# Two-block transformer on one core: side panels' weights split behind a unit's normalisation in the two-map attention

## The chip, the cores and the metric

The kernel runs on one core of a Trainium2 chip. The metric is the device time of one execution in microseconds; of several executions the median counts.

## The reference

256 tokens of width 1024 go through two blocks, all in float32. The first block (two layers: gated feed-forward, three kinds of attention, a second gated feed-forward) is not touched here. The second block computes, cut to what matters:

```
h = rmsnorm(x); p = h @ w_in
p_rwkv, p_mla, p_diff, p_gate = split(p)
o_rwkv = rwkv7_mix(p_rwkv)       # recurrent branch, with a group norm at its end
o_mla  = mla_mix(p_mla)          # latent attention, 8 heads
o_diff = diff_mix(p_diff)        # 4 heads; softmax of map 1 minus lambda * softmax of map 2
gates  = sigmoid(p_gate + b)     # 3 x 1024 columns
merged = sum over the branches of gate * (o_branch @ w_branch)
x = x + merged @ w_o; x = x + conv_ffn(rmsnorm(x)); return rmsnorm(x)
```

## The kernel before

**Panels and splits.** Every weight matrix is streamed from HBM in panels of 128 x 2048 floats. A float32 product is made of three fast ones (`three`, lines 1214 to 1216): high half of the weights by high half of the tokens, high by low, low by high. So a panel that has landed in `raw` must be split first: ScalarE (ACT) copies it to `whi` in the reduced format, VectorE (DVE) subtracts, which gives `wlo`. The rest of the kernel does this a whole panel at a time (`split`, lines 581 and 585). `split_piece` (lines 588 to 611) does it in four pieces: 0 and 2 are the two halves of `whi` (lines 598 and 600), 1 and 3 the two halves of `wlo` (both line 608). A panel's first matmul waits until piece 3 of that panel is done. The load of a panel into a `raw` slot waits until the slot's previous `wlo` is done.

**Side panels.** The projection `h @ w_in` has 27 panels of side work (`side_list`). They aren't multiplied in a stage of their own: they are put between the small, dependent steps of the branches, to fill the matmul engine (TensorE, PE). A panel is four quarters of 12 matmuls of 256 columns each. `dense(k)` issues the next k quarters. The generator `side_panels` issues for each quarter its matmuls (`side_quarter`), in a panel's quarter 0 also the copy of the panel before out of its bank (`side_flush`, `side_evac`, line 2249 for gate columns), and right behind the quarter the split of the next panel. From panel 16 on the split comes in pieces: behind quarter 0 piece 0, behind quarter 1 pieces 1 and 2, behind quarter 2 piece 3, behind quarter 3 none.

**Two-map attention.** `causal_attention` is a generator that takes one unit (a head and a block of 128 queries; 8 units) per turn. For unit i:

```
if n_maps == 2 and i + 1 < len(units):
    scores(i + 1)            # PE, at the head of turn i+1; both maps, banks 4 and 5
exponentials(i)              # DVE adds the bias map (L2886) and takes the maxima (L2798), ACT exponentials (L2800)
normalise(i - 1)             # DVE, L2809 to L2817
transposes(i - 2)            # PE (L2826), then an ACT copy (L2830)
values(i - 3)                # PE (L2890, L2891)
```

`scores(i + 1)` (L2879) waits for the exponentials of unit i, since both use banks 4 and 5. `transposes(i - 2)` waits for that unit's normalisation and for the copy of the transposes before.

**The order around the change.** The loop at the end of `second_block` takes 8 turns. In each: a unit's step; in turn 0 `dense(2)`; then one step of the recurrent branch's epilogue (`group_norm`) or, when that is over, of `mla_inputs` (the MLA heads' queries and keys: PE L2917 and L2919, ACT L2922 to L2928, DVE L2931 to L2935); then `dense(1 + i % 2 + (i == 1))`. When the loop starts, panel 16 has two quarters behind it. Panels 17, 18, 19 and 20 start in turns 0, 2, 5 and 7. Each engine works through its own instructions in the order in which they were issued, so what is written first also runs first on its engine.

Of the kernel before, what the change touches and what calls it, by code (L numbers as in the profile page):

```python
# [748 lines left out]
def build(nc, ins, out):  # L749
# [1420 lines left out]
    side_list = [("rwkv_in", k) for k in range(7)] + [("diff_in", k) for k in range(6)] + \  # L2170
                [("mla_in", k) for k in range(2)] + [("gate_in", k) for k in range(12)]
    s_side = nc.alloc_semaphore("side_panel_evacuated")
    mixed, side_at, side_quarters = {}, [0], [0]
# [14 lines left out]
    def side_quarter(n, q):  # L2188

        name, k = side_list[n]  # L2190
        g = PHASE[name].first + k
        slot, b = g % 2, q // 2
        if q == 0:
            pe.q.wait_ge(st.s_lo, g + 1)
            if n >= 3:
                pe.q.wait_ge(s_side, n - 1)
        if n == 0:
            for kc in range(2 * q, 2 * q + 2):
                r = high_first([(side_target(0, b), tile_of(slot, b * KC + kc), S) for b in range(2)], u_one, kc, ready[kc])[1]
        for kc in range(4 * (q % 2), 4 * (q % 2) + 4) if n else ():  # L2200
            if name == "diff_in" and k >= 4:
                w = (whi[slot][:, kc * 256:(kc + 1) * 256], wlo[slot][:, kc * 256:(kc + 1) * 256])
                r = three(side_target(n, b), chunk_of(u_one, kc, b * P, b * P + P), w, kc == 0, kc == KC - 1)
            else:
                r = three(side_target(n, b), tile_of(slot, b * KC + kc), chunk_of(u_one, kc, 0, S), kc == 0, kc == KC - 1)
        if q == 3:
            r.then_inc(st.s_pe, 1)
# [44 lines left out]
    def side_panels():  # L2252

        for n in range(len(side_list)):
            for q in range(4):
                side_quarter(n, q)
                if q == 0 and n >= 1:
                    side_flush(n)
                name, k = side_list[n + 1] if n + 1 < len(side_list) else ("branch", 0)
                if n < 16:  # L2260
                    if q == 0 and n > 0:
                        st.split(PHASE[name], Count(k))
                else:
                    for piece in ((0,), (1, 2), (3,), ())[q]:
                        st.split_piece(PHASE[name], k, piece)
                yield
        side_flush(len(side_list))

    def side_flush(n):

        if side_at[0] < n:
            side_evac(n - 1)
            side_at[0] = n

    side = side_panels()

    def dense(quarters):
        for _ in range(quarters):
            next(side, None)
            side_quarters[0] += 1  # L2280

    def side_done(name, k):
        n = side_list.index((name, k))
        assert side_at[0] > n, (name, k)
        return (s_side, n + 1)
# [29 lines left out]
    for i in range(4):  # L2315
        dense(2)
        x2 = scaled_rows("norm_final", [], range(2 * i, 2 * i + 2))
# [451 lines left out]
    def causal_attention(name, units, score, prepare, n_maps, pv, stat, free, probs, probs_t, twin, before):  # L2769


        mk = [dict() for _ in units]

        def score_bank(i, m):
            return banks[4 + m if n_maps == 2 else 4 + i % 2][:, 0:S]

        def scores(i):
            uu = units[i]
            j = i - 1 if n_maps == 2 else i - 2
            pe.after(mk[j]["exp"] if j >= 0 else before.get("exp"))  # L2780
            for m in range(n_maps):
                r = score(uu, m, score_bank(i, m))
            mk[i]["scores"] = pe.do(r)
            if name == "diff":
                gates_free[uu[0]] = gates_free[4 + uu[0]] = mk[i]["scores"]

        def exponentials(i):
            uu = units[i]
            qt = uu[-1]
            nk = (qt + 1) * P  # L2790
            k = i % 2
            st_ = stat[:, k, :]
            dve.after(mk[i]["scores"], mk[i - 2]["norm"] if i >= 2 else None)
            act.after(mk[i - N_PROBS]["transposed"] if i >= N_PROBS else None)
            for m in range(n_maps):
                bank = score_bank(i, m)
                dve.after(prepare(uu, m, bank))
                t = dve.do(dve.q.tensor_reduce(out=st_[:, m:m + 1], in_=bank[:, 0:nk], axis=AX.X, op=ALU.max, negate=True))  # L2798
                act.after(t)
                ex = act.do(act.q.activation(probs[i % N_PROBS][:, m, 0:nk], bank[:, 0:nk], ACT.Exp, bias=st_[:, m:m + 1],  # L2800
                                             accum_out=st_[:, 2 + m:3 + m]))
            mk[i]["exp"] = twin["exp"] = ex

        def normalise(i):
            nk = (units[i][-1] + 1) * P
            k = i % 2
            st_ = stat[:, k, :]
            dve.after(mk[i]["exp"])
            t = dve.do(dve.q.reciprocal(st_[:, 4:4 + n_maps], st_[:, 2:2 + n_maps]))  # L2809
            dve.after(t)  # L2810
            if n_maps == 2:
                t = dve.do(dve.q.tensor_tensor(st_[:, 5:6], st_[:, 5:6], lam[:, 3:4], ALU.mult))
                dve.after(t)
            t = dve.do(dve.q.tensor_scalar(probs[i % N_PROBS][:, 0, 0:nk], probs[i % N_PROBS][:, 0, 0:nk], st_[:, 4:5], None, ALU.mult))
            if n_maps == 2:
                dve.after(t)
                t = dve.do(dve.q.scalar_tensor_tensor(out=probs[i % N_PROBS][:, 0, 0:nk], in0=probs[i % N_PROBS][:, 1, 0:nk],  # L2817
                                                      scalar=st_[:, 5:6], in1=probs[i % N_PROBS][:, 0, 0:nk],
                                                      op0=ALU.mult, op1=ALU.add))
            mk[i]["norm"] = t  # L2820

        def transposes(i):
            qt = units[i][-1]
            pe.after(mk[i]["norm"], turned_free.get("copied"))
            for t in range(qt + 1):
                r = pe.q.transpose(banks[0][:, t * P:(t + 1) * P], probs[i % N_PROBS][:, 0, t * P:(t + 1) * P], cst("ident"))  # L2826
            mk[i]["transposed"] = pe.do(r)
            pair = i // 2
            act.after(mk[i]["transposed"], mk[2 * (pair - 2) + 1]["pv"] if pair >= 2 else None)
            mk[i]["copied"] = turned_free["copied"] = act.do(act.q.activation(  # L2830
                probs_t[pair % 2][:, 0:qt + 1, qt * P:(qt + 1) * P],
                banks[0][:, 0:(qt + 1) * P].rearrange("p (t q) -> p t q", t=qt + 1), ACT.Copy))

        def values(i):
            if units[i][-1] == 0:
                return
            pair = i // 2
            bank = banks[1][:, 0:S]
            pe.after(mk[i]["copied"], mk[i - 1]["copied"], turned_free.get("read"))
            r = pv(units[i], probs_t[pair % 2], bank)  # L2840
            mk[i]["pv"] = pe.do(r)
            if name == "diff":
                for t in range(2):
                    gates_free[8 + 2 * (pair // 2) + t] = mk[i]["pv"]
            free[pair] = turned_free["read"] = finish_head(name, units[i], bank, mk[i]["pv"])

        scores(0)
        for i in range(len(units) + 3):
            if n_maps == 1 and i + 1 < len(units):
                scores(i + 1)  # L2850
            if i < len(units):
                exponentials(i)
            if 1 <= i <= len(units):
                normalise(i - 1)
            if 2 <= i < len(units) + 2:
                transposes(i - 2)
            if i >= 3:
                values(i - 3)
            yield
            if n_maps == 2 and i + 1 < len(units):  # L2860
                scores(i + 1)
# [118 lines left out]
    def mla_pv(uu, pt, bank):  # L2980
# [10 lines left out]
    diff_heads = causal_attention("diff", diff_units, diff_score, diff_prepare, 2, diff_pv, diff_stat, diff_free,  # L2991
                                  diff_probs, diff_probs_t, last_of, {})
    builder = None
    for i in range(len(diff_units)):
        next(diff_heads)
        if i == 0:
            dense(2)
        if builder is None:
            if next(epilogue, "over") == "over":
                builder = mla_inputs()  # L3000
        if builder is not None:
            next(builder, None)
        dense(1 + i % 2 + (i == 1))
    mla_units = [(hh, qt) for hh in range(MH) for qt in range(2)]
    mla_heads = causal_attention("mla", mla_units, mla_score, mla_prepare, 1, mla_pv, mla_stat, mla_free,
                                 mla_probs, mla_probs_t, {}, last_of)
# [185 lines left out]
```

## Time and profile before

| | us |
|---|---|
| median of 3 runs | 2327.96 |
| the runs | 2321.61 to 2328.72 |
| the profiled execution, its own time | 2326.03 |
| its span, first to last instruction | 2324.7 |
| mean granted clock of TensorE in it | 0.989 |

Busy in the profiled execution: PE 2260.5 us, PE's weight loads 1920.7, DVE 1490.9, ACT 964.4, POOL 393.9. The attention that the change touches runs from 1945 to 1998 us of the span. A duration in the rows is that of one instruction or of a merged group; "idle before" is the time that the engine stood still ahead of it, and behind the arrow stands what ended that.

### The profile page before, as it was taken

The numbers are of one execution on the slowest core, as the hardware profiler recorded it, in microseconds if no ns is written. First come the engines' busy times: TensorE is split into PE (matmuls) and PEld (weight loads), VectorE is DVE, ScalarE is ACT, GpSimd is POOL, SyncE is SP. The second block draws the span as 40 slices with busy tenths as digits, with TensorE's granted clock in tenths as the row PEclk, the third lists the DMA queues.
The fourth block names the chain that finished last, engine by engine and source line by source line (L and its number), as shares of the span: only waits on it lengthen the run. The fifth ranks groups of instructions, "written<-read, shape, count | busy, mean of one in ns | idle before, by whom it ended". The sixth has DMA issues, their size and how long they took to land. (4 is left out here: it accounts for less than half of the span.)

```text
span 2324.7 us, 37251 instructions
## 1 busy us (share of the span) xinstructions
PE 2260.5 (97%) x14432; PEld 1920.7 (83%) x14432; DVE 1490.9 (64%) x2302; ACT 964.4 (41%) x1555; POOL 393.9 (17%) x381
## 2 busy tenths in 40 slices
PE   9999999999999999999999999989999999999998
PEld 6888887666778888888888876679998998898998
DVE  5756766465676666676564345666667766777874
ACT  5222224455442222242222244554446335656763
POOL 1000001100010000000000011049996575000000
PEclk9999999999999999999999999999999999999999
DMA  7654543311234444434443323124554332244544
GB/s 297 221 187 162 180 162 129 106 37 55 73 118 181 171 173 161 170 139 163 162 180 130 100 103 108 58 89 178 178 175 157 110 103 91 77 157 159 189 165 143
DMA packets 53911, 331.05 MB, mean 142 GB/s; under 512 B 6688, under 2 KB 7968, under 8 KB 23328
## 3 DMA queue, kind: packets, MB, share of 16 engines
q1 hardware_dynamic: 50336, 319.15, 38.6%
q0 software_dynamic: 3456, 10.25, 1.6%
q8 instruction: 83, 1.36, 0.2%
q14 instruction: 36, 0.29, 0.0%
HBM read 325.56 MB, written 3.80 MB: 142 GB/s over the span
## 5 line engine op out<-in xcount | busy, mean ns | idle before, releaser
L1214 PE MATMUL bank<-u_hi,whi 128*128 128x512 f32 (+1 forms) x2352 | 805.2, 342 | 4.8 <-ACT qT L1716 1.6
L1215 PE MATMUL bank<-u_lo,whi 128*128 128x512 f32 (+1 forms) x2352 | 789.7, 336 | 0.0
L1216 PE MATMUL bank<-u_hi,wlo 128*128 128x512 f32 (+1 forms) x2352 | 789.6, 336 | 0.0
L585 DVE TENSOR_TENSOR wlo<-raw,whi 128x2048 fp32r<-128x2048 f32 (+2 forms) x203 | 423.6, 2086 | 307.5 <-ACT whi L581 297.8
L1214 PEld LDWEIGHTS bank<-u_hi,whi 128*128 128x128 f32 x2352 | 443.1, 188 | 82.3 <-issue 27.8
L581 ACT ACTIVATE whi<-raw 128x2048 fp32r<-128x2048 f32 (+2 forms) x203 | 345.5, 1702 | 346.3 <-PE bank L1216 296.0
L1216 PEld LDWEIGHTS bank<-u_hi,wlo 128*128 128x128 f32 x2352 | 443.3, 188 | 47.5
L1215 PEld LDWEIGHTS bank<-u_lo,whi 128*128 128x128 f32 x2352 | 442.9, 188 | 44.6 <-issue 0.2
L1289 ACT ACTIVATE sil<-bank 128x512 f32<-128x512 f32 (+1 forms) x88 | 48.0, 545 | 519.4 <-PE bank L1216 516.6
L1214 PE MATMUL bank<-hidden_hi,whi 128*128 128x512 f32 x528 | 205.4, 389 | 0.0
L1215 PE MATMUL bank<-hidden_lo,whi 128*128 128x512 f32 x528 | 205.4, 389 | 0.0
L1216 PE MATMUL bank<-hidden_hi,wlo 128*128 128x512 f32 x528 | 205.4, 389 | 0.0
L643 POOL TENSOR_TENSOR wlo<-raw,whi 128x512 fp32r<-128x512 f32 x16 | 21.4, 1335 | 971.6 <-ACT whi L627 971.5
L943 DVE SCALAR_TENSOR_TENSOR bank<-raw,c_row 128x1024 f32<-128x1024 f32 x128 | 157.2, 1228 | 8.5 <-DMA raw<-in_stream 7.4
L1407 POOL TENSOR_TENSOR rel_bias_map<-rel_bias_map,bucket_step 128x384 f32<-128x384 f32 x124 | 158.1, 1275 | 10.4
L943 DVE SCALAR_TENSOR_TENSOR raw<-raw,bank 128x1024 f32<-128x1024 f32 x128 | 155.7, 1217 | 0.0
L1293 DVE TENSOR_TENSOR prod<-sil,bank 128x512 f32<-128x512 f32 (+1 forms) x88 | 54.6, 621 | 157.3 <-ACT sil L1289 154.3
L608 DVE TENSOR_TENSOR wlo<-raw,whi 128x1024 fp32r<-128x1024 f32 (+2 forms) x84 | 99.3, 1193 | 73.3 <-ACT whi L598 69.7
L1404 POOL TENSOR_SCALAR bucket_step<-in_bucket,bucket_steps 128x384 f32<-128x384 f32 x124 | 131.5, 1060 | 12.4
L1216 PEld LDWEIGHTS bank<-hidden_hi,wlo 128*128 128x128 f32 x528 | 99.1, 188 | 20.7
L1215 PEld LDWEIGHTS bank<-hidden_lo,whi 128*128 128x128 f32 x528 | 99.1, 188 | 20.6
L1214 PEld LDWEIGHTS bank<-hidden_hi,whi 128*128 128x128 f32 x528 | 99.1, 188 | 20.4
(450 smaller groups left out, 3204.9 us busy)
## 6 DMA issues: line engine op xcount, KB each, us to landing
raw<-in_stream SPq DMA_DIRECT2D x229, 1024.0 KB, 4.8
raw<-in_stream SPq DMA_DIRECT2D x80, 704.0 KB, 4.0
first_ada<-in_stream SPq DMA_DIRECT2D x8, 1024.0 KB, 16.7
raw<-in_stream SPq DMA_DIRECT2D x8, 768.0 KB, 4.2
skew<-rpb_rows POOLq DMA_DIRECT2D x8, 336.0 KB, 6.3
nbr_bias<-skew POOLq DMA_DIRECT2D x24, 112.0 KB, 5.9
h<-in_tokens SPq DMA_DIRECT2D x4, 512.0 KB, 5.6
raw<-in_stream SPq DMA_DIRECT2D x8, 256.0 KB, 16.8
```

The lines of the kernel that those rows point to most:

```text
L581: a.activation(self.hi[to][:, 0:n], raw[:, 0:n], ACT.Copy).then_inc(self.s_hi, 1)
L585: v.tensor_tensor(self.lo[to][:, 0:n], raw[:, 0:n], self.hi[to][:, 0:n].bitcast(F32), ALU.subtract).then_inc(self.s_lo, 1)
L608: r = v.q.tensor_tensor(self.lo[to][:, cols], self.raw[slot][:, cols], self.hi[to][:, cols].bitcast(F32), ALU.subtract)
L643: r = v.q.tensor_tensor(self.lo[to][:, cols], self.raw[slot][:, cols], self.hi[to][:, cols].bitcast(F32), ALU.subtract)
L943: r = dve.q.scalar_tensor_tensor(out=product, in0=w, scalar=1.0, in1=rows, op0=ALU.mult, op1=ALU.mult, accum_out=to)
L1214: pe.q.matmul(dst, w[0], x[0], start=start, stop=False)
L1215: pe.q.matmul(dst, w[0], x[1], start=False, stop=False)
L1216: return pe.q.matmul(dst, w[1], x[0], start=False, stop=stop)
L1289: act.q.activation(sil[par][:, 0:n], banks[2 * par][:, 0:n], ACT.Silu).then_inc(s_sil, 1)
L1293: dve.q.tensor_tensor(prod[par][:, 0:n], sil[par][:, 0:n], banks[2 * par + 1][:, 0:n], ALU.mult).then_inc(st.s_ev, 1)
L1404: z = pool.do(pool.q.tensor_scalar(step[:, :], bucket[:, :], 1.0 - start, steps[:, hh, b + 1:b + 2], ALU.add, ALU.mult))
L1407: z = pool.do(pool.q.tensor_tensor(rel[:, hh, :], rel[:, hh, :], step[:, :], ALU.add))
```

## The change

The splits leave `side_panels` and get a generator of their own, `side_splits`; `next_weights` catches it up with the quarters that have been issued. Outside the two-map attention `dense` calls it behind each quarter, as before. Within it (`weights_apart`) it is called in the next turn of `causal_attention`, behind `exponentials(i)` and `normalise(i - 1)` and ahead of `transposes(i - 2)`, and by `dense` ahead of a panel's quarter 0, since that panel's split must be issued by then.

```diff
--- before.py
+++ after.py
@@ -2256,6 +2256,13 @@
                 side_quarter(n, q)
                 if q == 0 and n >= 1:
                     side_flush(n)
+                yield
+        side_flush(len(side_list))
+
+    def side_splits():
+
+        for n in range(len(side_list)):
+            for q in range(4):
                 name, k = side_list[n + 1] if n + 1 < len(side_list) else ("branch", 0)
                 if n < 16:
                     if q == 0 and n > 0:
@@ -2264,7 +2271,6 @@
                     for piece in ((0,), (1, 2), (3,), ())[q]:
                         st.split_piece(PHASE[name], k, piece)
                 yield
-        side_flush(len(side_list))
 
     def side_flush(n):
 
@@ -2272,12 +2278,22 @@
             side_evac(n - 1)
             side_at[0] = n
 
-    side = side_panels()
+    side, side_weights, split_quarters, weights_apart = side_panels(), side_splits(), [0], [False]
+
+    def next_weights():
+
+        while split_quarters[0] < side_quarters[0]:
+            next(side_weights, None)
+            split_quarters[0] += 1
 
     def dense(quarters):
         for _ in range(quarters):
+            if side_quarters[0] % 4 == 0:
+                next_weights()
             next(side, None)
             side_quarters[0] += 1
+            if not weights_apart[0]:
+                next_weights()
 
     def side_done(name, k):
         n = side_list.index((name, k))
@@ -2852,6 +2868,8 @@
                 exponentials(i)
             if 1 <= i <= len(units):
                 normalise(i - 1)
+            if weights_apart[0]:
+                next_weights()
             if 2 <= i < len(units) + 2:
                 transposes(i - 2)
             if i >= 3:
@@ -2991,6 +3009,7 @@
     diff_heads = causal_attention("diff", diff_units, diff_score, diff_prepare, 2, diff_pv, diff_stat, diff_free,
                                   diff_probs, diff_probs_t, last_of, {})
     builder = None
+    weights_apart[0] = True
     for i in range(len(diff_units)):
         next(diff_heads)
         if i == 0:
@@ -3001,6 +3020,8 @@
         if builder is not None:
             next(builder, None)
         dense(1 + i % 2 + (i == 1))
+    weights_apart[0] = False
+    next_weights()
     mla_units = [(hh, qt) for hh in range(MH) for qt in range(2)]
     mla_heads = causal_attention("mla", mla_units, mla_score, mla_prepare, 1, mla_pv, mla_stat, mla_free,
                                  mla_probs, mla_probs_t, {}, last_of)
```

In the rows of order that follow, line numbers of the change are 16 (epilogue) or 18 (attention) above those of before for the same code. `wlo<-raw,whi` on DVE is piece 1 or 3, `whi<-raw` on ACT piece 0 or 2.

DVE, between unit 0's and unit 1's mask addition, where panel 17 starts (`token_roots` and `inverse_t` belong to the epilogue's group norm). Before:

```order
L2886 TENSOR_TENSOR bank<-bank,rel_bias_map 128x128
L2798 TENSOR_REDUCE diff_stat<-bank 128x1
L608 TENSOR_TENSOR wlo<-raw,whi 128x1024
L2735 RECIPROCAL token_roots<-token_roots 128x16
L2737 COPY inverse_t<-token_roots 128x1024
L2886 TENSOR_TENSOR bank<-bank,rel_bias_map 128x256
```

Now:

```order
L2904 TENSOR_TENSOR bank<-bank,rel_bias_map 128x128
L2814 TENSOR_REDUCE diff_stat<-bank 128x1
L2751 RECIPROCAL token_roots<-token_roots 128x16
L2753 COPY inverse_t<-token_roots 128x1024
L608 TENSOR_TENSOR wlo<-raw,whi 128x1024
L2904 TENSOR_TENSOR bank<-bank,rel_bias_map 128x256
```

The last piece of panel 17 went from ahead of the reciprocal and the copy to behind them.

DVE around unit 2 (`diff_probs_14222` is unit 1's), where panel 18 starts. Before:

```order
L2746 TENSOR_TENSOR mixed<-mixed,bonus 128x1024
L608 TENSOR_TENSOR wlo<-raw,whi 128x1024 x2
L2886 TENSOR_TENSOR bank<-bank,rel_bias_map 128x128
L2798 TENSOR_REDUCE diff_stat<-bank 128x1
...
L2809 RECIPROCAL diff_stat<-diff_stat 128x2
L2812 TENSOR_TENSOR diff_stat<-diff_stat,lambda 128x1
L2814 TENSOR_SCALAR diff_probs_14222<-diff_probs_14222,diff_stat 128x256
L2817 SCALAR_TENSOR_TENSOR diff_probs_14222<-diff_probs_14222,diff_stat 128x256
L2749 TENSOR_TENSOR mixed<-mixed,g 128x1024
```

Now:

```order
L2762 TENSOR_TENSOR mixed<-mixed,bonus 128x1024
L2904 TENSOR_TENSOR bank<-bank,rel_bias_map 128x128
L2814 TENSOR_REDUCE diff_stat<-bank 128x1
...
L2825 RECIPROCAL diff_stat<-diff_stat 128x2
L2828 TENSOR_TENSOR diff_stat<-diff_stat,lambda 128x1
L2830 TENSOR_SCALAR diff_probs_14222<-diff_probs_14222,diff_stat 128x256
L2833 SCALAR_TENSOR_TENSOR diff_probs_14222<-diff_probs_14222,diff_stat 128x256
L608 TENSOR_TENSOR wlo<-raw,whi 128x1024 x2
L2765 TENSOR_TENSOR mixed<-mixed,g 128x1024
```

Both pieces of panel 18 went behind unit 2's additions and maxima and unit 1's normalisation. In the same way the two pieces of panel 19 go behind unit 4's maxima and unit 3's normalisation, the first of panel 20 behind unit 6's and 5's, and its last behind unit 7's and 6's.

ACT in turn 6 (`diff_probs_14221` is unit 6's, L2830 or L2846 the copy of unit 4's transposes). Before:

```order
L2249 ACTIVATE gates_h<-bank,vec_49 128x256 x2
L598 ACTIVATE whi<-raw 128x1024
L600 ACTIVATE whi<-raw 128x1024
L2800 ACTIVATE diff_probs_14221,diff_stat<-bank,diff_stat 128x128 x2
L2830 ACTIVATE diff_probs_t_14224<-bank 128x128
```

Now:

```order
L2249 ACTIVATE gates_h<-bank,vec_49 128x256 x2
L2816 ACTIVATE diff_probs_14221,diff_stat<-bank,diff_stat 128x128 x2
L598 ACTIVATE whi<-raw 128x1024
L600 ACTIVATE whi<-raw 128x1024
L2846 ACTIVATE diff_probs_t_14224<-bank 128x128
```

Panel 20's `whi` went from ahead of unit 6's exponentials to between them and the copy.

## Rows read from the trace of the kernel before

**Rows 1.** Page, busy time, share of the span and instructions of an engine.
```profile
PE 2260.5 (97%) x14432; PEld 1920.7 (83%) x14432; DVE 1490.9 (64%) x2302; ACT 964.4 (41%) x1555; POOL 393.9 (17%) x381
```

**Rows 2.** Waits of PE, 1944 to 2000: us in total, times, longest.
```profile
PE bank L2879 <- ACT diff_probs L2800: 3.1, 3, 1.6
PE bank L1214 <- DVE wlo L608: 1.4, 2, 1.0
...
PE bank L2973 <- ACT mla_probs L2800: 1.0, 1, 1.0
PE bank L2973 <- ACT diff_probs L2800: 0.6, 1, 0.6
```

**Rows 3.** Timeline of PE: start, us, instruction, idle time before it.
```profile
1948.37 1.84 PE L2391 MATMUL bank<-const,v_tokens 128*128 128x2 f32 x16
1950.08 0.36 PE L1214 MATMUL bank<-u_hi,whi 128*128 128x256 f32 x1
...
1958.52 0.49 PE L2879 MATMUL bank<-gates_h 64*128 64x128 f32 x4
...
1960.25 0.39 PE L1214 MATMUL bank<-u_hi,whi 128*128 128x256 f32 x1 [0.97 <-DVE wlo L608]
...
1968.17 0.49 PE L2879 MATMUL bank<-gates_h 64*128 64x128 f32 x4 [0.69 <-ACT diff_probs L2800]
...
1973.18 0.70 PE L2879 MATMUL bank<-gates_h 64*128 64x256 f32 x4 [0.79 <-ACT diff_probs L2800]
...
1978.08 0.49 PE L2879 MATMUL bank<-gates_h 64*128 64x128 f32 x4
...
1983.77 0.70 PE L2879 MATMUL bank<-gates_h 64*128 64x256 f32 x4 [1.58 <-ACT diff_probs L2800]
...
1987.61 0.38 PE L1214 MATMUL bank<-u_hi,whi 128*128 128x256 f32 x1 [0.43 <-DVE wlo L608]
...
1998.09 0.70 PE L2973 MATMUL bank<-mla_k,mla_q 96*128 96x256 f32 x2 [1.03 <-ACT mla_probs L2800]
```

**Rows 4.** Stretch behind it: us, busy PE, PEld, DVE, ACT, POOL; clock, DMA, GB/s.
```profile
2000.00:2050.00 50.00, 49.81 (x374) 45.79 (x374) 34.74 (x82) 30.07 (x71) 0.00 (x0) 0.97 0.31 111
```

**Rows 5.** Timeline of DVE, same columns as rows 3.
```profile
1947.10 1.53 DVE L608 TENSOR_TENSOR wlo<-raw,whi 128x1024 fp32r<-128x1024 f32 x1
...
1951.24 0.78 DVE L2737 COPY inverse_t<-token_roots 128x1024 f32<-128x1024 f32 x1
...
1957.84 2.35 DVE L608 TENSOR_TENSOR wlo<-raw,whi 128x1024 fp32r<-128x1024 f32 x2
1960.11 0.29 DVE L2886 TENSOR_TENSOR bank<-bank,rel_bias_map 128x128 f32<-128x128 f32 x1
...
1961.17 0.16 DVE L2809 RECIPROCAL diff_stat<-diff_stat 128x2 f32<-128x2 f32 x1
...
1962.35 1.22 DVE L2749 TENSOR_TENSOR mixed<-mixed,g 128x1024 f32<-128x1024 f32 x1
...
1973.84 0.43 DVE L2931 COPY mla_k<-bank 64x256 f32<-64x256 f32 x1
...
1975.73 0.43 DVE L2886 TENSOR_TENSOR bank<-bank,rel_bias_map 128x256 f32<-128x256 f32 x1
```

**Rows 6.** Timeline of ACT and DVE ahead of unit 6's addition.
```profile
1980.69 1.06 ACT L600 ACTIVATE whi<-raw 128x1024 fp32r<-128x1024 f32 x1
...
1980.83 1.22 DVE L608 TENSOR_TENSOR wlo<-raw,whi 128x1024 fp32r<-128x1024 f32 x1 [1.00 <-ACT whi L598]
```

**Rows 7.** Timeline of PE ahead of a fall of the clock; three stretches, columns of rows 4.
```profile
1796.62 1.92 PE L2391 MATMUL bank<-const,v_tokens 128*128 128x2 f32 x16 [0.43 <-ACT v_tokens L2375]
...
1948.00:1952.00 4.00, 4.00 (x37) 3.83 (x35) 1.64 (x3) 3.96 (x10) 3.63 (x5) 1.00 0.51 166
...
1799.10:1802.40 3.30, 3.30 (x18) 3.30 (x17) 2.05 (x2) 2.86 (x3) 0.00 (x0) 0.50 0.00 0
...
1981.00:1985.00 4.00, 2.42 (x19) 1.80 (x18) 3.75 (x11) 2.90 (x10) 0.00 (x0) 1.00 0.00 0
```

**Rows 8.** Page, DMA issues: KB each, median us from issue to landing.
```profile
raw<-in_stream SPq DMA_DIRECT2D x229, 1024.0 KB, 4.8
```

## The prediction

> **What bounds the kernel now.** I read the page first, then the waits of the matmul engine, then the timelines of three engines around the change. The page says that TensorE (PE) is busy for 97% of the span [rows 1], so whatever leaves PE idle is what can be won or lost. All that the change touches lies between 1945 and 2000 us. There PE waits four ways: three times for the exponentials that must release banks 4 and 5 before the next scores, twice for the low half of a side panel's weights (`wlo`), and twice where the MLA scores follow exponentials [rows 2]. In order of time these waits are 0.97 us at 1960.25, 0.69 at 1968.17, 0.79 at 1973.18, 1.58 at 1983.77, 0.43 at 1987.61, 0.64 ahead of the first MLA scores and 1.03 at 1998.09 [rows 2, 3]. They sum to 6.1 us, 0.26% of the span, which is the most that any order of VectorE and ScalarE could win here. Behind it, from 2000 to 2050 us, PE is busy for 49.8 of 50 us [rows 4], so a shift that PE has at 1998 is carried to the end.
>
> **What the change moves.** No instruction is added or removed and PE, POOL and SP keep their order. On VectorE (DVE) and ScalarE (ACT) the pieces of a side panel's split go from behind their quarter, thus ahead of the next unit's mask addition, row maximum and exponentials, to behind that unit's exponentials and the previous unit's normalisation. What matters is the due time of the piece that moves. A panel's first matmul waits for its last `wlo` piece. Four panels start here, 17 to 20, at 1950.08, 1960.25, 1974.82 and 1987.61.
>
> **Panel 17: +3.2 us.** Before, `wlo` ran at 1947.10, while DVE had nothing else, and was done 1.4 us before PE came [rows 3, 5]. Now it is queued behind the reciprocal and the copy to `inverse_t`, which wait for a square root of sums that PE makes at 1948.37, and the copy ends at 1951.24 + 0.78 = 1952.02 [rows 5]. With 1.22 us for the piece (the row before took 1.53 at 1947.10, the upper bound; two others share 2.35) and 0.06 us from DVE to PE (1960.19 to 1960.25), PE starts at 1953.3 in place of 1950.1 [rows 3, 5, 6]. That is 3.2 us, 3.5 with the upper bound. Nothing covers it.
>
> **Panel 18: +3.5 us.** Before, the two pieces ran at 1957.84, ahead of unit 2's addition; PE waited 0.97 us for them [rows 3, 5]. Now DVE first needs unit 2's scores, which PE issues just ahead of the panel. Scores start at 1958.52 + 3.2 = 1961.7 and end 0.5 later; additions and maxima take 1.06 (1960.11 to 1961.17), the normalisation 1.18 (to 1962.35), the two pieces 2.35 [rows 5]: 1966.9. PE starts there in place of 1960.25, so the shift is 6.7 and the wait 4.5 us. ScalarE's second half fits in: it stands behind exponentials that end near 1963.9 and takes 1.06 [rows 6].
>
> **What comes back: -0.7 and -0.8 us.** The waits at 1968.17 and 1973.18 go [rows 3]. For the first, the exponentials ended 5.75 us behind the start of L2749 at 1962.35 [rows 3, 5]; now that starts at 1966.9 and they end at 1972.7, while PE arrives at 1967.5 + 6.7 = 1974.2. For the second, unit 4's addition no longer stands behind two pieces. Shift 5.2.
>
> **Panel 19: 0, unit 6's scores: +0.5.** The two pieces, behind unit 3's normalisation, end near 1979.5; PE comes at 1974.8 + 5.2 = 1980.0. But they now stand ahead of the four MLA operations (1973.84 to 1975.73, 1.9 us) and unit 5's addition [rows 5]. From unit 4's scores at 1974.2: 0.5 + 1.1 + 1.2 + 2.4 + 1.9, then 1.6 for unit 5's 256 columns and 0.7 to the end of the exponentials make 1983.7, against PE's arrival at 1978.0 + 5.2 = 1983.2. Shift 5.7.
>
> **Unit 7's scores: -1.6, its transposes: +0.8.** The longest old wait, 1.58 us at 1983.77, came from `wlo` waiting for `whi` and holding up unit 6's addition [rows 3, 6]. It goes. But ScalarE's two `whi` halves, 1.06 us each and some 2.0 together [rows 6], now stand ahead of the copy that frees bank 0 for the next transposes, and PE is there first. Shift 4.9.
>
> **Panel 20: +2.6.** Unit 6's addition starts at 1985.6 (DVE is busy until then), its exponentials end at 1987.2, `whi` at 1988.3, the first piece at 1989.5, MLA operations at 1991.4, unit 7's maxima at 1993.0, the normalisation at 1994.1 and the last piece at 1995.3. PE starts panel 20 at 1995.1 to 1995.4 in place of 1987.61 [rows 3]: a wait of 3.0 in place of 0.43, shift 7.5. **MLA scores: -0.6 and -0.5**: of 0.64 and 1.03 the first goes and half of the second [rows 2, 3]. DVE and ACT run late by the same time as PE from there.
>
> **The sum of waits** is 3.2 + 3.5 - 1.5 + 0.5 - 1.6 + 0.8 + 2.6 - 1.1 = +6.4 us. I give it 1 us either way. Loads stay covered: a panel's load is issued when `wlo` has read its slot and takes 4.8 us [rows 8], and no load's panel is split here earlier than 7 us behind that, by the times above.
>
> **The clock.** At 1799.1 the granted clock stands at 0.50 (1.2 GHz) for a row of 3.3 us, behind 0.43 us of waiting and 1.92 us of two-column matmuls; the wait of 1.58 us at 1983 and the same small matmuls at 1948.37 left it at 1.00 [rows 7]. The new waits are 3.2 us (right behind those small matmuls), 4.5 and 3.0, longer than all that left the clock alone. A row of 3.3 us at half clock costs 1.65 us of PE's work where PE is what is waited for, and after the first two it is. Bounds for three falls: 0 (none, or wholly inside the waits) and 5.0 (three whole ones). I take 1.0 each, since part of a fall lies in its own wait: +3.0. The Trainium skill (TensorE: Matmul & The Clock Gate, section HAM oscillation) says that a loop whose PE waits between bursts starts the next burst cold, and counts the loss as half of the throttled time. By that rule all three falls are paid; it agrees with the halved clock of the row at 1799.
>
> Sum: the profiled execution's 2326.0 + 6.4 + 3.0 = 2335.4. The median of the runs shown, 2328.0, is 1.9 above that execution; I set the forecast half that way, at **2336.4**. A measurement of this kernel can tell about 0.3%, 7.0 us, from no change, and the forecast is 8.4 above the median.
>
> **Rivals.**
> - The waits grow as worked out and the clock does not fall (17%): +6.4, 2332.4 to 2334.4. For it: 1.58 us left the clock alone. Against: each new wait is twice that.
> - The clock stays down longer behind each wait (8%): twice the 3.3 us, +6.4 + 6 to 7, about 2339.5 to 2342.
> - The late panels are made good later (8%): the MLA units that follow could have slack in which DVE catches up, leaving +3, 2329 to 2331. Against it: PE is busy for all but 0.2 us of the 50 behind 2000 [rows 4], so there is next to no wait to shorten.
> - The other side (3%): the pieces are not late. If the last `wlo` of a panel came before PE did, only the waits for exponentials would go: -(0.7 + 0.8 + 1.6 + 0.6 + 1.0) = -4.7, 2321.3 to 2323.3. It decides at one point: whether panel 17's `wlo` is done by 1950.1 and panel 18's by 1959.3. Both now stand behind work that starts at 1951.2 and after unit 2's scores, so the rows speak against it.
> - The change does not do what it says (2%): 2326 to 2328. The order of the rows shows that it does.
> - My forecast, waits and falls (62%): 2333.5 to 2339.
>
> **Chances.** Slower by over 7 us, above 2335: about 0.55 of the forecast's 0.62, 0.08 of long falls and 0.05 of the first rival, 0.68. Faster 0.03. The rest 0.29. The range runs from 2331, which leaves out most of the catching up and the gain, to 2341.
>
> **What would show it.** In the profile after: PE waits for `wlo` L608 with some 11 us in three waits, of 3, 4.5 and 3 us, where it had 1.4; its waits for `diff_probs` fall from 3.1 to under 1; `wlo` stands behind the copy to `inverse_t`; and the clock is at 0.50 in one to three rows between 1953 and 2003. Wrong would be the first wait under 1 us, which ends the argument; or all three waits there and the clock at 1.00, which leaves +6.4; or PE idle less behind 2000 us than before.

## The result, and the profile after

The change made the kernel slower: 2339.11 us in the median of 6 runs against 2324.39 before (6 runs), a ratio of 1.0060 with a 95% interval of 1.0046 to 1.0074. Two later comparisons, each on a chip of its own, gave 1.0061 (1.0044 to 1.0077) and 1.0060 (1.0046 to 1.0074). So the change costs 14 to 15 us in each of the three (14.7, 14.1 and 15.1). The profiled execution took 2335.8 us, 9.8 more than the one of before.

The page of the kernel after, its busy times, answers to [rows 1]:

```profile
span 2334.5 us, 37251 instructions
...
PE 2264.6 (97%) x14432; PEld 1925.3 (82%) x14432; DVE 1489.7 (64%) x2302; ACT 964.3 (41%) x1555; POOL 393.4 (17%) x381
```

The instructions are the same. PE is busy for 4.1 us longer with the same matmuls, which is a first sign of a slower clock. The waits of PE in the kernel after, from 1944 to 2012 us (total, times, longest), answer to [rows 2]:

```profile
PE bank L1214 <- DVE wlo L608: 11.2, 3, 4.4
...
PE bank L2842 <- ACT diff_probs_t L2846: 0.9, 1, 0.9
PE bank L2897 <- ACT diff_probs L2816: 0.6, 1, 0.6
PE bank L2991 <- ACT mla_probs L2816: 0.4, 1, 0.4
```

What the change was to shorten did shrink: the waits for `diff_probs` ahead of scores went from 3.1 to 0.6 us. But PE now waits 11.2 us for `wlo` where it waited 1.4. The timeline of PE in the kernel after shows each, as [rows 3] do:

```profile
1955.36 0.58 PE L1214 MATMUL bank<-u_hi,whi 128*128 128x256 f32 x1 [3.72 <-DVE wlo L608]
...
1971.55 0.58 PE L1214 MATMUL bank<-u_hi,whi 128*128 128x256 f32 x1 [4.44 <-DVE wlo L608]
...
1989.44 0.49 PE L2897 MATMUL bank<-gates_h 64*128 64x128 f32 x4 [0.59 <-ACT diff_probs L2816]
...
1995.07 0.41 PE L2842 MATMUL bank<-const,diff_probs 128*128 128x128 f32 x2 [0.89 <-ACT diff_probs_t L2846]
...
2000.83 0.38 PE L1214 MATMUL bank<-u_hi,whi 128*128 128x256 f32 x1 [3.07 <-DVE wlo L608]
```

These are panels 17, 18 and 20, unit 6's scores and unit 5's transposes. The timeline of DVE after, which answers to [rows 5], shows why:

```profile
1952.37 0.25 DVE L2751 RECIPROCAL token_roots<-token_roots 128x16 f32<-128x16 f32 x1 [3.77 <-ACT token_roots L2749]
1952.66 0.98 DVE L2753 COPY inverse_t<-token_roots 128x1024 f32<-128x1024 f32 x1
1953.56 1.74 DVE L608 TENSOR_TENSOR wlo<-raw,whi 128x1024 fp32r<-128x1024 f32 x1
...
1969.14 2.35 DVE L608 TENSOR_TENSOR wlo<-raw,whi 128x1024 fp32r<-128x1024 f32 x2
```

DVE stands idle for 3.77 us while panel 17's piece is queued behind the reciprocal; before, the same piece had run ahead of this idle time, so its input was ready. The clock is the second part. The granted clock tells at which share of 2.4 GHz PE was allowed to run. Four stretches of the kernel after (us, busy PE, PEld, DVE, ACT, POOL, then PE's granted clock, DMA share, GB/s), to be read beside [rows 7]:

```profile
1944.00:1958.00 14.00, 8.88 (x61) 8.22 (x59) 7.39 (x13) 6.72 (x11) 10.90 (x13) 0.86 0.09 28
1958.00:1975.00 17.00, 12.56 (x79) 10.82 (x77) 12.16 (x25) 5.89 (x14) 0.00 (x0) 0.81 0.23 84
1975.00:2000.00 25.00, 21.28 (x142) 17.83 (x140) 20.70 (x56) 15.18 (x44) 0.00 (x0) 1.00 0.16 55
2000.00:2012.00 12.00, 10.72 (x62) 9.69 (x63) 8.46 (x21) 6.47 (x17) 0.00 (x0) 0.86 0.23 88
```

A mean of 1.00 is full clock throughout. The other three lie below it, so part of each was run at 1.2 GHz: three falls, one around each wait for `wlo` (the first reaches from the first stretch into the second).

**A measure for what follows.** A single execution scatters by several us, and most of that arises elsewhere in the program. So I also use the marked stretch: on PE's timeline, from the start of unit 0's scores to the start of the MLA scores that wait at 1998.09 in [rows 3]. Before it is 1998.09 - 1945.02 = 53.07 us, after it is 65.00. There is one profile of before, and its clock was at 1.00 for the whole of this stretch.

### The profile page after: what moved, and what is told of

Read it like the earlier page. It is cut to its first block and busy times, and to the rows that moved or that the text cites. A ratio compares the mean times of both kernels' runs of the same rounds, so it can differ in the third digit from the quotient of the medians.

```text
span 2334.5 us, 37251 instructions
## 1 busy us (share of the span) xinstructions
PE 2264.6 (97%) x14432; PEld 1925.3 (82%) x14432; DVE 1489.7 (64%) x2302; ACT 964.3 (41%) x1555; POOL 393.4 (17%) x381
```

## The experiments

Each was compared with the kernel before on the same chip. The theory has two parts: W, late `wlo` pieces make PE wait, +6.4 us; C, falls of the clock around these waits come on top.

**The change again** (no edit).

> The change once more, on the chip that the three kernels sent with it run on. Theory W+C (late wlo pieces add 6.4 us of waits of PE, and the clock falls that follow them add 3 to 5): +9 to +12 us against the kernel before; three waits for wlo of 3.7, 4.4 and 3.1 us in the trace. Theory W alone (the rest of the measured 14.7 us is the scatter of single executions): +6 to +7.

2340.38 us against 2326.29, ratio 1.0061; marked stretch 64.38, that is +11.3. W alone is out: its +6 to +7 lies below the interval, which starts at 1.0044, 10.2 us. W+C's +9 to +12 reaches into it, though it ends below the 14.1 measured; the stretch's +11.3 lies within W+C.

**Panel 17's piece put back.**

```diff
     for i in range(len(diff_units)):
         next(diff_heads)
+        weights_apart[0] = False
         if i == 0:
             dense(2)
+        weights_apart[0] = i in (0, 1, 2, 3, 4, 5, 6, 7)
```

(Here and in the variants below, `causal_attention` calls `next_weights()` for every unit of the two-map attention.)

> The change, but the last piece of panel 17 stays behind its quarter, ahead of the epilogue's reciprocal and copy. Theory W: the wait of 3.7 us at panel 17 is gone, panel 18 keeps its wait of some 4.4 us, panel 20 its 3, and the sum of waits is +3.1 us against before. Theory W+C: one stretch of 1.2 GHz fewer too, +4.5 to +7 against before, 4 to 6 less than the whole change. Rival (the shift is made later by something else, say by exponentials that collide with whi): no more than 1 us less than the whole change.

2332.48 us, ratio 1.0027 (1.0016 to 1.0039), marked stretch 57.85: +4.8. Its waits of PE, 1940 to 2018:

```profile
PE bank L1214 <- DVE wlo L608: 7.5, 2, 4.4
```

One of three waits is gone, the other two have kept their size. This single piece was worth 6.5 to 7.2 us of the stretch (64.38 and 65.00 less 57.85) and 7.9 of the median, where 4 to 6 were expected. The rival, that the shift would be made later by something else, falls. Panel 20's wait, which ends at 1995.78 here, left the clock alone, so two of the three falls went with this piece and not the one that was expected:

```profile
1992.00:2003.00 11.00, 7.92 (x56) 7.30 (x56) 9.06 (x23) 7.01 (x18) 0.00 (x0) 1.00 0.25 96
```

**All three late pieces put back**: turn 0's first quarters, turn 1 (panel 18) and turn 6 (panel 20's last piece). Panel 19's split and panel 20's first three pieces stay moved.

```diff
+        weights_apart[0] = False
         if i == 0:
             dense(2)
+        weights_apart[0] = i in (0, 2, 3, 4, 5, 7)
```

> The change without its three late pieces: panel 17's and 18's splits and panel 20's last piece stay behind their quarters; panel 19's split and panel 20's first three pieces stay moved. Theory W: no wait for wlo over 1 us, the waits of 0.79 and 1.58 us for exponentials are gone, one wait of 0.9 for the copy of the transposes comes; -0.8 us against before, which is not to be told from no change. If moving the splits as such costs (ACT's order of whi and exponentials), it stays slower by over 3 us.

2324.69 us against 2326.29, ratio 0.9997 (0.9987 to 1.0007), marked stretch 52.11: -0.96 where -0.8 was worked out. Waits of PE, 1940 to 2018:

```profile
PE bank L1214 <- DVE wlo L608: 1.6, 2, 1.1
PE bank L2842 <- ACT diff_probs_t L2846: 1.6, 2, 0.8
...
PE bank L2991 <- ACT mla_probs L2816: 1.0, 1, 1.0
PE bank L2897 <- ACT diff_probs L2816: 0.7, 1, 0.7
PE bank L2991 <- ACT diff_probs L2816: 0.6, 1, 0.6
```

So the moves that are not late cost nothing that can be told. They turn 2.4 us of waits for exponentials into 1.6 us of waits for the copy of the transposes, which stands behind `whi` on ACT. The whole slowdown belongs to the three late pieces.

**PE kept busy where it would wait.** 26, 34 and 24 products whose result nobody reads:

```diff
+        if q == 0 and n in keep_busy:
+            pe.after(turned_free["read"])
+            for _ in range(keep_busy[n]):
+                z = pe.q.matmul(banks[1][:, 0:S], u_one[0][:, 0, 0:P], u_one[0][:, 0, 0:S], start=True, stop=True)
+            pe.do(z)
```

> The change with 26, 34 and 24 products of 256 columns that nobody reads put into bank 1 ahead of panels 17, 18 and 20, so that PE works where it would wait; each takes 0.12 us at 2.4 GHz, 3.1, 4.0 and 2.8 us in all, less than the waits. What is computed stays the same. Theory W+C: the granted clock stays at 1.00 from 1950 to 2000, PE's waits shrink to under 0.7 us each, panels start where the waits alone put them, and the time is +6.4 us against before, 2 to 5 less than the whole change. Theory W alone: as slow as the whole change, within 1 us.

2332.16 us, ratio 1.0023 (1.0012 to 1.0034), marked stretch 59.40: +6.33 against a worked out +6.4. The same four stretches:

```profile
1944.00:1958.00 14.00, 12.60 (x96) 11.47 (x95) 9.77 (x20) 8.88 (x17) 12.64 (x16) 1.00 0.01 1
1958.00:1975.00 17.00, 16.07 (x131) 14.82 (x132) 12.53 (x25) 5.47 (x13) 2.27 (x2) 1.00 0.21 69
1975.00:2000.00 25.00, 23.52 (x161) 20.06 (x162) 21.48 (x57) 16.00 (x46) 0.00 (x0) 1.00 0.21 80
2000.00:2012.00 12.00, 11.36 (x78) 10.33 (x77) 9.95 (x24) 7.03 (x18) 0.00 (x0) 1.00 0.26 89
```

The clock stays at 1.00 throughout, the late pieces are as late as before, and 84 useless matmuls made the kernel 8.2 us faster than the bare change (2340.38 to 2332.16). The time was expected 2 to 5 us below the whole change; it is 8.2 below. This separates W from C: the waits alone cost 6.3 us of the stretch and 5.9 of the median, and what comes on top when PE stands idle in them is 5.0 to 5.6 of the stretch and 8.2 of the median.

**One late piece alone**, in the order of before, bare and filled:

```diff
+        weights_apart[0] = True
         if i == 0:
             dense(2)
+        weights_apart[0] = i in ()
```

> The kernel before with one piece moved: panel 17's last wlo stands behind the epilogue's reciprocal and copy. Theory W+C: a wait of 3.7 us ahead of panel 17, behind it 3.4 to 6.8 us at 1.2 GHz; from unit 0's scores to the last marked MLA scores (53.1 us before) 3.2 to 3.7 us of waits and 2 to 3 of clock, +5.5 to +6.5, and the time +4 to +7 us. Theory W alone: +3.2 to +3.7 in both. Rival (DVE and ACT have slack behind it and catch up): under +2 by the marked scores.

> The same one moved piece, with 26 products of 256 columns that nobody reads put into bank 1 ahead of panel 17. What is computed stays the same. Theory W+C: the same due time of wlo, PE's wait shrinks to 0.6 us, no fall of the clock behind it, and the marked stretch is +3.2 to +3.7 us, 2 to 3 less than without the products. Theory W alone: no difference between the two.

Bare: 2334.93 us, ratio 1.0035 (1.0021 to 1.0048), marked stretch 58.73, +5.7. Filled: 2328.09 us, ratio 1.0006 (0.9997 to 1.0015), marked stretch 56.97, +3.9. PE's wait in the bare form:

```profile
1951.97 0.58 PE L1214 MATMUL bank<-u_hi,whi 128*128 128x256 f32 x1 [3.73 <-DVE wlo L608]
```

The stretch agrees with W+C: 3.9 for the wait and 1.8 for the clock, a little over the expected 3.2 to 3.7 and under the expected 2 to 3. There is no slack up to the mark, so the rival falls. The times fit less well. The bare form's +7.7 us lies above the expected +4 to +7, and between the two medians lie 6.8 us, not 1.8. (The profiled execution of the bare form, 2324.27 us, was the fastest of its six.) The filled form's time came out below its stretch, +0.8 us with an interval from -0.7 to +3.5, and why is open. More on both behind the last experiment.

**Panel 20 alone**: turn 6 stays moved, turn 0's first quarters and turn 1 are put back (`weights_apart[0] = i in (0, 2, 3, 4, 5, 6, 7)`).

> The change with panel 17's and 18's splits left behind their quarters; panel 19's split and all of panel 20's stay moved. Theory W: one late piece is left, panel 20's last, with a wait of 2.5 to 3 us for it; the marked stretch is +0.8 us against before where the kernel without that move had -0.96, so the piece costs 1.8. With C up to 1.7 more if the clock falls behind it; time +1 to +3 us. Rival (panel 20's lateness comes only from being shifted by the earlier two): no wait over 1 us there.

2327.60 us against 2327.25, ratio 1.0001 (0.9992 to 1.0010), marked stretch 56.08, +3.0. PE waits 3.1 us for panel 20's `wlo`, so this lateness is its own and not inherited; the rival falls. The stretch is 2.2 us over the waits' +0.8, where up to 1.7 was expected of the clock. The clock went down around the wait and stayed down for the whole of this row:

```profile
1992.00:1999.00 7.00, 6.10 (x23) 5.55 (x24) 3.77 (x10) 3.13 (x8) 0.00 (x0) 0.51 0.45 151
```

The timed runs show none of it: +0.3 us with an interval from -1.9 to +2.3, where +1 to +3 was expected and the stretch has +3.0. What one late piece costs in the median of this kernel is at the edge of what can be told.

**`wlo` on POOL.** The order of before, but for panels 19 to 21:

```diff
-        a, v = self.e.A, self.e.V
+        on_pool = ph.name == "gate_in" and k in (4, 5, 6)
+        a, v = self.e.A, self.e.G if on_pool else self.e.V
```

> The order of before, but the low halves of panels 19, 20 and 21 are subtracted on POOL, which has nothing to do from 1955 us on, in place of DVE. A piece of 1024 columns is 2.7 us there if it scales from the 1.34 us of 512 columns. Theory (DVE's queue is what the exponentials of this stage wait for): PE's waits of 0.79, 1.58, 0.43, 0.64 and 1.03 us shrink by 2.5 to 4 us together, the stretch is that much shorter and the time 2 to 4 us less than before. Rival (POOL's pieces come too late, or slow DVE down): waits for wlo at panels 19 to 21 of over 1 us, or DVE's operations of this stage longer than before, and no gain.

2329.02 us against 2327.25, ratio 1.0010 (1.0001 to 1.0020), marked stretch 56.01, +2.9. The theory failed. Of the rival the first half is out, since PE waits for no `wlo` of panels 19 to 21, and the second half holds: POOL's pieces slow DVE down. The timelines of POOL, DVE and PE in it:

```profile
1985.98 4.98 POOL L611 TENSOR_TENSOR wlo<-raw,whi 128x1024 fp32r<-128x1024 f32 x2 [8.00 <-ACT whi L599]
...
1986.22 2.15 DVE L2833 TENSOR_TENSOR diff_stat<-diff_stat,lambda 128x1 f32<-128x1 f32 x1
...
1988.79 2.44 DVE L2838 SCALAR_TENSOR_TENSOR diff_probs<-diff_probs,diff_stat 128x256 f32<-128x256 f32 x1
...
1991.29 0.44 PE L2847 MATMUL bank<-const,diff_probs 128*128 128x128 f32 x2 [2.99 <-DVE diff_probs L2838]
```

A product of one column, 0.16 us elsewhere, takes 2.15 and ends halfway through POOL's two pieces. The next operation with two inputs in SBUF takes 2.44 in place of 0.48 and ends 0.3 us behind the second piece. PE waits 2.99 us for it. The next longest wait, 2.40 us at the mark, stands behind two more such operations, of 2.48 and 2.25 us.

**The bare and the filled change once more, and the version without late pieces.**

> The change once more, beside its filled form on the same chip: what is still open is whether the falls of the clock cost the 5.3 us that the marked stretch shows (11.3 to 11.9 against 6.3 filled) or the 8.2 us between the medians. Theory (the loss is made in the stretch): marked stretch +11 to +12 against before, 5 to 6 more than filled, and the medians of both sets of runs pooled differ by 5 to 6. Rival (falls elsewhere in the program are changed too): the medians differ by 8 or more again.

> The filled form of the change once more. Waits alone: marked stretch +6.3 us, no stretch at 1.2 GHz in it, time +6 us against before. Rival: a time that is less than +4 or more than +8.

> The change without its three late pieces once more, to see if it beats the kernel before. Theory: marked stretch -0.9 us, time -0.5 to -1.5 us, with the earlier -0.7 us (0.9987 to 1.0007) still not to be told from no change. Rival (fewer falls of the clock as well): -2 us or more.

Against 2326.30 before: the change 2341.38, ratio 1.0060 (1.0046 to 1.0074); filled 2331.29, 1.0017 (1.0008 to 1.0027); without late pieces 2324.50, 0.9990 (0.9980 to 1.0001). Marked stretches 67.19, 59.30 and 52.09. The medians of the change and of its filled form differ by 10.1 us here, after 8.2 in the first comparison. The theory of 5 to 6 us, all of it lost in the stretch, is thereby not confirmed; the number named for the rival, 8 or more, came instead. Whether the rival's reason holds, that falls elsewhere in the program change too, can be looked up in the profiles. From the mark to the end of the span they took:

| | us |
|---|---|
| before | 326.6 |
| filled, two profiles | 326.5, 326.6 |
| the change, three profiles | 323.1, 325.0, 325.7 |
| panel 17 alone, bare and filled | 321.2, 324.9 |

So falls elsewhere do change, but in these profiles they favour the bare change: a fall that stands 15 to 16 us behind the mark before and in both filled profiles is in none of its three. From unit 0's scores to the end of the span the bare change took 8.4, 9.7 and 13.2 us more than before, the filled form 6.2 twice. That makes the difference between the medians no easier to explain. It does bear on the runs with one late piece, by one profile each: at the end of the span panel 17 alone, filled, and panel 20 alone were both 2.2 us over before, in place of 3.9 and 3.0 at the mark, and 2.2 lies within both of their intervals. In this profile of the change the stretches around the three waits were slower still:

```profile
1944.00:1958.00 14.00, 8.88 (x60) 8.16 (x60) 6.68 (x13) 6.72 (x11) 10.18 (x13) 0.81 0.14 47
1958.00:1975.00 17.00, 12.55 (x80) 10.59 (x78) 12.50 (x26) 5.89 (x14) 0.00 (x0) 0.80 0.22 86
1975.00:2000.00 25.00, 21.49 (x139) 17.67 (x138) 20.05 (x55) 14.98 (x43) 0.00 (x0) 0.97 0.12 43
2000.00:2012.00 12.00, 10.95 (x57) 10.16 (x58) 7.30 (x17) 5.51 (x13) 0.00 (x0) 0.72 0.25 88
```

With waits of 11.2 us for `wlo` as in the other profiles, the stretch is 14.1 us over before here, 11.3 and 11.9 there. The waits repeat to 0.1 us; what varies is how long the clock stays down.

## Why the prediction was right, and where its size was off

The forecast was slower, 2336.4 us in a range of 2331 to 2341; the median was 2339.1, and 2340.4 and 2341.4 in the two later comparisons, the last of them just above the range. The kind of loss and its two parts were right. The size of the change was not as close as these times look: +9.4 us was added up and +14.7 measured, and 2.6 us of the gap were hidden by a base that was too high, which is luck. The filled form shows the waits without the clock, so that each step can be read off. Starts of scores on PE, counted from unit 0's:

| scores of | before | change, filled | difference | worked out |
|---|---|---|---|---|
| unit 1 (behind panel 17's start) | 6.64 | 10.56 | +3.9 | +3.2 |
| unit 3 (behind panel 18's start) | 16.84 | 24.07 | +7.2 | +6.7 |
| unit 4 | 23.15 | 29.61 | +6.5 | +6.0 |
| unit 5 | 28.16 | 33.66 | +5.5 | +5.2 |
| unit 6 | 33.06 | 39.02 | +6.0 | +5.7 |
| unit 7 | 38.75 | 43.06 | +4.3 | +4.1 |
| first MLA scores (behind panel 20's) | 44.91 | 51.94 | +7.0 | +6.9 |
| the mark | 53.07 | 59.40 | +6.3 | +6.4 |

- **Panel 17, "+3.2 us": right in kind, 0.5 to 0.7 too small.** The wait was 3.7 us. The copy took 0.98 and not 0.78, the piece 1.74 and not 1.22, over my upper bound of 1.53. POOL was at work at the same time (next section). From unit 5 on the surplus is down to 0.1 to 0.3 us.
- **Panel 18, "+3.5", the two that come back, unit 6's "+0.5", unit 7's "-1.6", the transposes' "+0.8", panel 20's "+2.6"**: measured +3.5 (from 3.76 at unit 2 to 7.23), -0.8, -1.0, +0.5, -1.7, a wait of 0.89, and a wait of 3.07 where 3.0 was worked out. The rule behind all of them, that a piece's place counts by its panel's start and not by its quarter, held.
- **"The sum of waits, +6.4 us"**: 6.33 and 6.2 in the two filled profiles. That the whole shift is carried to the end held for them (6.2 of it); of the bare change's, up to 3.5 us came back behind the mark, as above.
- **"The clock, +3.0": the mis-sized term.** Over the filled form the bare change's stretch is 5.0, 5.6 and 7.8 us longer (64.38, 65.00, 67.19 against 59.35). My upper end of 5.0 was too low. I took each fall as one row of 3.3 us at 0.50, as at 1799 in [rows 7], though the falls here lasted up to twice that, and the kernel before had held a longer one to read, earlier in the program:

```profile
1560.20:1570.00 9.80, 8.10 (x31) 6.99 (x32) 8.47 (x10) 6.69 (x14) 8.88 (x11) 0.50 0.00 0
```

By the granted clock of the four stretches, 0.86, 0.81, 1.00 and 0.86 in the first profile make (14 x 0.14 + 17 x 0.19 + 12 x 0.14) x 2 = 13.7 us at 1.2 GHz, the second profile has 13.7 as well, and 0.81, 0.80, 0.97 and 0.72 in the last make 20.3 us. The rival with long falls, which I gave 8%, described that last profile, and the medians of 2340.4 and 2341.4 lie in its range as well; that of 2339.1 lies between its range and that of my forecast row, 2333.5 to 2339. What a fall costs can be worked out from where it lies. A slow clock costs nothing while PE waits anyway, and this is the first fall in the kernel after, in the last 1.3 us of the wait and behind it:

```profile
1954.00:1955.30 1.30, 0.00 (x0) 0.00 (x0) 1.30 (x1) 0.37 (x1) 1.30 (x2) 0.56 0.00 0
1955.40:1960.80 5.40, 5.40 (x22) 4.53 (x23) 1.24 (x4) 0.39 (x2) 0.49 (x1) 0.50 0.52 194
```

Of the 13.7, 13.7 and 20.3 us at 1.2 GHz in the three profiles, 1.6, 2.6 and 3.6 lay within the waits; half of the rest is 6.0, 5.5 and 8.4, against 5.6, 5.0 and 7.8 measured. So "part of a fall lies in its own wait" was right, but it takes off 0 to 1 us from a fall's cost, and what I had too small was the length of the falls. Half of the throttled time, the price in the Trainium skill (TensorE: Matmul & The Clock Gate, section HAM oscillation), would be 6.9, 6.9 and 10.2 us. The traces agree with the half to 0.6 us, once the time within waits is left out.

- **The base.** The median before was 2324.4 to 2327.3 in four comparisons, and the forecast stood on 2327.0 (2336.4 less 9.4). That is 2.6 us above the 2324.4 of the first comparison, which hid part of the error in the clock, and within 0.7 us of the other three.

Between the medians of bare and filled lie 8.2 and 10.1 us, more than the 5.0 to 7.8 of the three profiles. The mean granted clock of the change's 12 runs in two comparisons is 0.984, that of the filled form's 19 runs 0.988, as before; times two times 2340 us that is 75 against 56 us at 1.2 GHz. The 19 us more are as much as the longest of the three profiles had in the stretch, and worth up to 9.5 us. So the clock is what differs in the timed runs too. That they had long falls in the stretch more often than the profiled ones is a guess, and where their falls lie was not shown, since timed runs leave no rows.

The version without the three late pieces is the only one that comes out ahead of before, by 1.6 and 1.8 us in two medians and 1.0 us in the stretch. The stretch shows the gain twice; in the time it can't be told from none.

## What to carry to other kernels

When work is moved on an in-order engine, list for each piece who waits for it and by when, and compare that with what now stands ahead of it, the waits of that work included: here one piece of 1.2 us, put behind a reciprocal that waits for another engine, made the matmul engine wait for 3.7 us. A wait on the matmul engine can be paid twice, since the clock may fall around it: price it as the wait plus half of the time at the lower clock that falls on work, and take the longest falls in the trace, not the first one found. If such a wait can't be avoided, matmuls that nobody reads can pay: here they gave back over half of the loss.

## What the runs showed of the hardware

**VectorE stands still while GpSimd works, for operations with two inputs in SBUF.** Beside the rows above, the timeline of POOL in the kernel after shows what made panel 17's piece 1.74 us long:

```profile
1953.17 2.72 POOL L2463 TENSOR_TENSOR rel_bias_map<-rel_bias_map,tables 128x256 f32<-128x256 f32 x2
```

The same two instructions took 1.42 us before. So both engines were slowed, by 1.3 and 0.5 us, where they met. The 1.53 us at 1947.10 in [rows 5] is such a meeting too, with this row of POOL before, which ends 0.44 us behind its start; I had read it as scatter.

```profile
1946.53 1.01 POOL L1407 TENSOR_TENSOR rel_bias_map<-rel_bias_map,bucket_step 128x384 f32<-128x384 f32 x1
```

Operations with an input in a bank of PSUM went on. With a piece on POOL from 1975.60 to 1977.98, the timeline of DVE in the variant with `wlo` on POOL has:

```profile
1975.74 0.29 DVE L2909 TENSOR_TENSOR bank<-bank,rel_bias_map 128x128 f32<-128x128 f32 x1
...
1976.47 1.52 DVE L2833 TENSOR_TENSOR diff_stat<-diff_stat,lambda 128x1 f32<-128x1 f32 x1
```

The first keeps its 0.29 us, the second, with both inputs in SBUF and 0.16 us long elsewhere, ends with the piece. The copy to `inverse_t`, from SBUF to SBUF with one input, grew too, from 0.78 to 0.98 us, with POOL at work both times. The Trainium skill (SBUF — State Buffer, section SBUF: two separate sides) says that the pair of ports that VectorE and GpSimd share is locked for a whole instruction; the runs agree, 0.16 us having become 2.15.

**Falls of the clock around equal waits differ in length, and one wait had none.** The waits of 3.7, 4.4 and 3.1 us were the same in three profiles. Over 2000 to 2012 us the granted clock was 0.86 in the first and 0.72 in the last. In the variant with panel 17's piece put back the wait of 3.08 us for panel 20 left the clock at 1.00 from 1992 to 2003. With PE fed in the same places it was 1.00 in both filled profiles.
